# Constants, modulation head, norm, features and the q, k, v projection in one stage

## The reference

```python
cs = jax.nn.silu(c)
mod = cs @ ada_w[l] + ada_b[l]                       # 1024 -> 6 * 1024
sh1, sc1, gt1, sh2, sc2, gt2 = split(mod, 6)
h = rmsnorm(x, norm_g[l, 0]) * (1.0 + sc1) + sh1
z = h @ mix_in[e]                                    # 1024 -> 3584
qb, kb, vb = split(z[..., 2048:], 3, -1)             # 512 columns each
qb = rope(qb, pos); kb = rope(kb, pos)
```

## Time and profile before

| | |
|---|---|
| median of 3 runs | 2945.14 us (2944.81, 2945.14 and one of 3172.86) |
| profiled execution | 2942.27 us, its span 2940.4 us |
| mean granted TensorE clock | 0.951 |
| busy in the span | TensorE 2632.1, VectorE 1587.1, ScalarE 1127.0, GpSimd 943.1 us |
| first load of the columns, of the head, of x, of the q, k, v stage | 2.25, 12.03, 50.08, 91.68 us |
| first instruction of the stage behind | 275.83 us |

### The profile page before, as it was taken

How to read it: one execution, slowest core, us unless ns; L and a number is a source line. 1 busy time by engine, 2 the same in 40 slices (tenths; PEclk the granted TensorE clock), 3 DMA queues, 4 the chain that set the end, 5 groups by cost and what they waited for, 6 DMA issues and landing times. The chain is left out here.

```text
span 2940.4 us, 54937 instructions
## 1 busy us (share of the span) xinstructions
PE 2632.1 (90%) x23160; PEld 2148.2 (73%) x23160; DVE 1587.1 (54%) x2286; ACT 1127.0 (38%) x1791; POOL 943.1 (32%) x645
## 2 busy tenths in 40 slices
PE   2688999796899999996999999999797999999998
PEld 0466755464889888775888888877575888888887
DVE  4565642255565454564655556445745655556445
ACT  1311243353333333343444444445343444444434
POOL 0510212101112111212777772000232677774000
PEclk7899999898999999998999999999798999999999
DMA  5556634602311211322222226643132222225654
GB/s 174 183 198 221 209 129 179 215 21 62 89 46 53 83 46 68 109 73 72 74 85 79 86 86 220 193 157 126 67 108 86 65 86 86 76 82 186 204 186 148
DMA packets 299010, 346.50 MB, mean 118 GB/s; under 512 B 31485, under 2 KB 227290, under 8 KB 298766
## 3 DMA queue, kind: packets, MB, share of 16 engines
q1 hardware_dynamic: 289118, 336.65, 35.3%
q10 hardware_dynamic: 9648, 6.34, 0.7%
HBM read 271.59 MB, written 71.35 MB: 117 GB/s over the span
## 5 line engine op out<-in xcount | busy, mean ns | idle before, releaser
L2835 POOL TENSOR_TENSOR cg_u_lo<-cg_u_raw,cg_u_hi 128x512 fp32r<-128x512 f32 x216 | 328.0, 1526 | 139.2 <-ACT cg_u_hi L2721 139.2
L307 PE MATMUL cg_ps<-m_hi,cg_u_hi 128*128 128x512 f32 x844 | 331.7, 393 | 32.7 <-POOL cg_u_lo L2835 28.4
L309 PE MATMUL cg_ps<-m_hi,cg_u_lo 128*128 128x512 f32 x844 | 330.4, 392 | 0.0
L308 PE MATMUL cg_ps<-m_lo,cg_u_hi 128*128 128x512 f32 x808 | 316.1, 391 | 0.0
L2721 ACT ACTIVATE cg_u_hi<-cg_u_raw 128x512 fp32r<-128x512 f32 x216 | 132.2, 629 | 387.4 <-PE cg_ps L309 235.1
L307 PEld LDWEIGHTS cg_ps<-m_hi,cg_u_hi 128*128 128x128 f32 x844 | 159.9, 189 | 68.0 <-POOL cg_u_lo L2835 29.2
L2885 DVE SCALAR_TENSOR_TENSOR cg_z<-cg_ps,top_conv_f,cg_z 128x1023 f32<-128x1023 f32 x88 | 112.9, 1283 | 137.1 <-ACT cg_z L2745 137.1
L307 PE MATMUL cg_ps<-over_y_tx,cg_u_hi 128*128 128x512 f32 x480 | 186.8, 389 | 0.0
L308 PE MATMUL cg_ps<-over_y_tx,cg_u_hi 128*128 128x512 f32 x480 | 186.8, 389 | 0.0
L309 PE MATMUL cg_ps<-over_y_tx,cg_u_lo 128*128 128x512 f32 x480 | 186.8, 389 | 0.0
L309 PEld LDWEIGHTS cg_ps<-m_hi,cg_u_lo 128*128 128x128 f32 x844 | 159.8, 189 | 33.5
(11 more groups left out here) (468 smaller groups left out, 6492.2 us busy)
## 6 DMA issues: line engine op xcount, KB each, us to landing
cg_u_raw<-in_ffn_up SPq DMA_DIRECT2D x88, 512.0 KB, 5.4
cg_u_raw<-in_ffn_down SPq DMA_DIRECT2D x64, 512.0 KB
qkv_mw<-in_ada_w SPq DMA_DIRECT2D x12, 2048.0 KB
over_f_d_raw<-in_ffn_down SPq DMA_DIRECT2D x48, 512.0 KB
scr_act<-cg_z SPq DMA_DIRECT2D x44, 512.0 KB, 2.7
mod_w<-in_ada_w SPq DMA_DIRECT2D x8, 1024.0 KB
za_w_raw<-in_mix_in SPq DMA_DIRECT2D x16, 512.0 KB, 4.9
za_out<-in_ada_w SPq DMA_DIRECT2D x8, 1024.0 KB
```

What stands on the lines that cost most here:

```text
L307: nc.tensor.matmul(out, a_hi, b_hi, start=first, stop=False)
L308: nc.tensor.matmul(out, a_hi, b_lo, start=False, stop=False)
L309: return nc.tensor.matmul(out, a_lo, b_hi, start=False, stop=last)
L2835: G.tensor_tensor(u_lo[:, n % RING], source(g, i), u_hi[:, n % RING].bitcast(F32), ALU.subtract).then_inc(ulo_done, 1)
```

## The change

The five stages become one, `features_and_qkv`, without a barrier in between. `columns` has 19 groups: the biases of shift and scale and the norm's gain come as columns too. SP loads in the order of `HEAD_ORDER`: halves of head chunks and pairs of token tiles in turns, the 19 groups behind chunk 1. The head uses the stream's two weight slots. VectorE adds up one chunk at a time and scales a token tile when its turn comes. The sum over partitions takes the accumulator as weights, 128 columns at a time, against the column of ones, so shift and scale arrive as columns in PSUM and do not pass through HBM. Inverse roots come from a root on ScalarE and a reciprocal on VectorE. TensorE turns each token tile by itself, ScalarE evicts it to `xt`. Gain and shift are applied to whole rows of 1024 tokens, on ScalarE for h_hi and on VectorE for h32, and VectorE alone makes h_lo. h_hi lies over x, h_lo over xt. The rope tables are loaded behind w_raw 3. TensorE multiplies the first four tiles together, k by k as the low parts come.

```diff
-def modulation_head(nc, c, ada_w, ada_b, mod_d, consts):
...
-def norm_to_features(nc, name, x_src, norm_row, mod_row, at, consts, h_hi, h_lo):
...
-def project_qkv(nc, mix_in, h_hi, h_lo, consts, rope_cos, rope_sin, qk_d, v_d, ada_w, ada_b, mod_d):
+def features_and_qkv(nc, x_src, cond, mix_in, columns, x, xt, h_hi, h_lo, consts, rope_cos, rope_sin, qk_d, v_d, ada_w, ada_b, mod_d):
...
+            rows, sq = o.sb("rows", [max(sizes), 24, P]), o.sb("sq", [P, D])
+            h32 = Scope(nc, octx, "over_rope").sb("h32", [P, 4, D])
+        mps = s.ps("mps", [P, 2, CHUNK])
+        ms = ModulationStream(nc, s, 2, consts, modulation_room(s, 2) + (mps,))
-        ms = ModulationStream(nc, s, 2, consts, modulation_room(s, 2) + (s.ps("mps", [P, 2, CHUNK]),))
...
+        def x_bank(t):
+            return ps[:, 2 * (t % 2):2 * (t % 2) + 2, :].rearrange("p a (f c) -> p (a f) c", c=P)
+        HEAD_ORDER = [("w", 0, 0), ("w", 0, 1), ("x", 0), ("x", 1), ("w", 1, 0), ("w", 1, 1), ("x", 2), ("x", 3), ("w", 2, 0), ("w", 2, 1),
+                      ("x", 4), ("x", 5), ("w", 3, 0), ("x", 6), ("x", 7), ("w", 3, 1)]
...
             def load_chunk(c):
                 if c < 2:
                     sp.wait_ge(ms.pad_clear, 1)
+                    sp.wait_ge(row_done, HEAD * KT)
                 else:
                     sp.wait_ge(ms.acc_done, c - 1)
                 l, e = chunk_of(c)
                 ms.load(sp, ada_w[l].rearrange("(t p) (e n) -> e p t n", p=P, n=CHUNK)[e],
                         ada_b[l, e * CHUNK:(e + 1) * CHUNK].rearrange("(o n) -> o n", o=1), c % 2)
-            sp.dma_start(cos[:, :, :], rope_cos.rearrange("(t p) e -> p t e", p=P)).then_inc(tab_loaded, 16)
-            sp.dma_start(sin[:, :, :], rope_sin.rearrange("(t p) e -> p t e", p=P)).then_inc(tab_loaded, 16)
+            def head_chunk(j, half):
+                k = slice(half * KH, (half + 1) * KH)
+                if j >= 2:
+                    sp.wait_ge(row_done, (j - 2) * KT + (half + 1) * KH)
+                sp.dma_start(ms.w[:, j % 2, k], ada_w[0].rearrange("(t p) (e n) -> e p t n", p=P, n=CHUNK)[j][:, k]).then_inc(head_loaded[j][half], 16)
+            sp.dma_start(ccol[:, :], cond.rearrange("o (t p) -> p (o t)", p=P), allow_slow_non_contiguous=True).then_inc(c_loaded, 16)
+            for n, (kind, *at) in enumerate(HEAD_ORDER):
+                if kind == "w":
+                    head_chunk(*at)
+                else:
+                    sp.dma_start(x[:, at[0], :], x_src[at[0] * P:(at[0] + 1) * P, :]).then_inc(x_loaded[at[0]], 16)
+                if n == 5:
+                    for i, (src, _) in enumerate(columns):
+                        sp.dma_start(rows[0:sizes[i], i, :], src).then_inc(cols_loaded[i], 16)
             for n in range(NC * KT):
                 cb, k = divmod(n, KT)
...
                 if n >= R:
                     sp.wait_ge(lo_done, n - R + 1)
                 sp.dma_start(w_raw[:, n % R, :], w_v[k, :, 4 * WA + cb * WA:4 * WA + (cb + 1) * WA]).then_inc(raw_loaded[n % R], 16)
+                if n == R - 1:
+                    sp.dma_start(cos[:, :, :], rope_cos.rearrange("(t p) e -> p t e", p=P)).then_inc(tab_loaded, 16)
+                    sp.dma_start(sin[:, :, :], rope_sin.rearrange("(t p) e -> p t e", p=P)).then_inc(tab_loaded, 16)
                 if n == 2 * KT - 1:
                     for c in range(4):
                         load_chunk(c)
...
         def _(act):
+            A = nc.scalar.activation
+            def weight_high(cb, k):
+                n = cb * KT + k
+                act.wait_ge(raw_loaded[n % R], 16 * (n // R + 1))
+                A(w_hi[:, cb % 2, k, :], w_raw[:, n % R, :], ACT.Copy).then_inc(hi_done, 1)
-                    nc.scalar.activation(w_hi[:, cb % 2, k, :], w_raw[:, n % R, :], ACT.Copy).then_inc(hi_done, 1)
+                    weight_high(cb, k)
+            def square(t):
+                act.wait_ge(x_loaded[t], 16)
+                if t:
+                    act.wait_ge(ss_done, t)
+                A(sq[:, :], x[:, t, :], ACT.Square, accum_out=ss[:, t:t + 1]).then_inc(ss_done, 1)
+                act.wait_ge(ss_done, t + 1)
+                A(root[:, t:t + 1], ss[:, t:t + 1], ACT.Sqrt, scale=1.0 / D, bias=eps[:, :]).then_inc(root_done, 1)
+            def evict(t):
+                act.wait_ge(xs_turned, t + 1)
+                A(xt[:, :, t * P:(t + 1) * P], x_bank(t), ACT.Copy).then_inc(xt_done, 1)
+            def feature_high(f):
+                act.wait_ge(gain_done, 1)
+                act.wait_ge(shift_done, 1)
+                A(h_hi[:, f, :], xt[:, f, :], ACT.Identity, scale=gain[:, f:f + 1], bias=shift[:, f:f + 1]).then_inc(fhi_done, 1)
             def stage_out(cb, t):
                 n = cb * TT + t
...
+            act.wait_ge(eps_set, 1)
+            for t in range(TT):
+                square(t)
+                if t:
+                    evict(t - 1)
+            evict(TT - 1)
+            for k in range(R):
+                weight_high(0, k)
+            act.wait_ge(xt_done, TT)
+            for f in range(KT):
+                feature_high(f)
+                if f + R < KT:
+                    weight_high(0, f + R)
             split(1)
             for cb in range(NC):
                 for t in range(TT):
...
         @block.gpsimd
+            nc.gpsimd.memset(ident[:, :], 0.0).then_inc(zeroed, 1)
+            nc.gpsimd.memset(eps[:, :], RMS_EPS).then_inc(eps_set, 1)
+            pool.wait_ge(zeroed, 1)
+            nc.gpsimd.affine_select(out=ident[:, :], in_=ident[:, :], compare_op=ALU.not_equal, fill=1.0, base=0,
+                                    pattern=[[-1, P]], channel_multiplier=1).then_inc(ident_set, 1)
+            for n in range(NC * KT):
+                cb, k = divmod(n, KT)
+                pool.wait_ge(hi_done, n + 1)
+                nc.gpsimd.tensor_tensor(w_lo[:, cb % 2, k, :], w_raw[:, n % R, :], w_hi[:, cb % 2, k, :].bitcast(F32),
+                                        ALU.subtract).then_inc(lo_done, 1)
...
+            def head_rows(j, half):
+                dve.wait_ge(head_loaded[j][half], 16)
+                acc = ms.acc[:, j % 2, :]
+                for k in range(half * KH, (half + 1) * KH):
+                    w = ms.w[:, j % 2, k, :]
+                    if k:
+                        dve.wait_ge(row_done, j * KT + k)
+                        V.scalar_tensor_tensor(acc, w, silu[:, k:k + 1], acc, ALU.mult, ALU.add).then_inc(row_done, 1)
+                    else:
+                        if j >= 2:
+                            dve.wait_ge(chunk_summed, j - 1)
+                        V.tensor_scalar(acc, w, silu[:, 0:1], None, ALU.mult).then_inc(row_done, 1)
+            def scale_x(t):
+                dve.wait_ge(root_done, t + 1)
+                V.reciprocal(rstd[:, t:t + 1], root[:, t:t + 1]).then_inc(rstd_done, 1)
+                dve.wait_ge(rstd_done, t + 1)
+                V.tensor_scalar(x[:, t, :], x[:, t, :], rstd[:, t:t + 1], None, ALU.mult).then_inc(xs_done, 1)
+            def copy_columns():
+                dve.wait_ge(cols_turned, len(columns))
+                for i, (_, dst) in enumerate(columns):
+                    V.tensor_copy(dst, pt[:, 0, starts[i]:starts[i] + sizes[i]]).then_inc(cols_copied, 1)
+            def feature_low(f):
+                dve.wait_ge(h32_done, f + 1)
+                dve.wait_ge(fhi_done, f + 1)
+                V.tensor_tensor(h_lo[:, f, :], h32[:, f % 4, :], h_hi[:, f, :].bitcast(F32), ALU.subtract).then_inc(flo_done, 1)
             def chunk_rows(c):
                 dve.wait_ge(ms.loaded[c % 2], 32 * (c // 2 + 1))
                 if c >= 2:
                     dve.wait_ge(ms.sum_done, c - 1)
+                else:
+                    dve.wait_ge(chunk_summed, HEAD)
...
                 for k in range(KT):
                     ms.add_row(dve, c, c % 2, k)
+            V.memset(ones[:, :], 1.0).then_inc(ones_set, 1)
+            V.memset(heads[:, :], 0.0).then_inc(heads_zeroed, 1)
+            dve.wait_ge(heads_zeroed, 1)
+            V.memset(heads[0:HD, 0:HD], 1.0)
...
+            for n, (kind, *at) in enumerate(HEAD_ORDER):
+                if kind == "w":
+                    head_rows(*at)
+                else:
+                    scale_x(*at)
+                if n == 9:
+                    copy_columns()
+            dve.wait_ge(chunk_summed, HEAD)
+            dve.wait_ge(cols_copied, len(columns))
+            V.tensor_tensor(shift[:, :], mps[:, 0, 0:KT], shift_b[:, :], ALU.add).then_inc(shift_done, 1)
+            V.tensor_tensor(scale[:, :], mps[:, 0, KT:2 * KT], scale_b[:, :], ALU.add).then_inc(scale_done, 1)
+            dve.wait_ge(scale_done, 1)
+            V.scalar_tensor_tensor(gain[:, :], scale[:, :], 1.0, g[:, :], ALU.add, ALU.mult).then_inc(gain_done, 1)
+            dve.wait_ge(gain_done, 1)
+            dve.wait_ge(xt_done, TT)
+            for f in range(KT):
+                if f >= 4:
```

(59 more changed lines are left out.)

265 lines of the change are left out of this document (41 added, 224 removed).

## The result

The changed kernel takes 2911.26 us (median of four runs, 2908.25 to 2916.52) against 2945.14 of the kernel before (three runs, 2944.81 to 2948.07): 33.9 us less. The ratio is 0.9881, with a 95% interval of 0.9862 to 0.9900. That is 1.2% less, and by the 2% of the forecast no change. A fourth run of the kernel before, 3172.86 us in a slower state of the chip, is left out of all of this. The profiled execution took 2908.25 us with a span of 2906.5, against 2942.27 and 2940.4: 34 us less. The forecast was 2899, from a gain of 46.0 us at tile 4.

The account below looks back on a forecast made before the run. Serialization of five stages bounds until 108.5 us, then TensorE. First product gains 57.6 us, a new hole takes back nearly 12: 46.0 off 2942.27 gives 2896.3, plus 2.9 to the median, 2899; range 2886 to 2914.

Parts of the forecast that it names:

- the new hole: Before tile 4: TensorE idle some ten us, behind chunk 0's load and rows and rope 2; takes back nearly 12 us.
- low parts over 2.7 us apart: Sign of a wrong forecast, in the features: low parts coming slower than TensorE's 2.7 us for one k.
- Transfers and the head: Start to gain: transfers end at 37.1, VectorE and ScalarE bind, last half chunk ends at 45.6, gain at 47.5.
- rival (c): Head: late slot gates stall SP's stream, column sums cost 2.6 us more; gain 32 to 35, median 2910 to 2913; chance 0.11.
- Features: Behind the gain: low parts every 1.9 us, TensorE starts at 50.9, 57.6 us earlier, and is never held again.
- the lock: Features: VectorE operations wait for GpSimd's w_lo; one wait a pair makes the period 3.2, tile 4 1.8 us later.
- Four tiles: First four token tiles on TensorE: 4 x 5.45 us plus 1.7 lost at low clock, done at 74.4.
- Behind tile 4: Tile 4 to stage's end: same waits, 141 us; the chunk 4 hole moves along, could at most vanish (8.7 us).
- (d): TensorE stays at 1.2 GHz behind the hole before tile 4; for all 20 tiles 52 us slower, 2997; chance 0.03.
- rival (b): Features and head: VectorE waits for GpSimd, root and evictions later; 2 to 6 us lost, median 2901 to 2905; 0.70 with forecast.
- rival (a): VectorE follows transfers, chunk 0 in time, clock high at both starts: tile 4 at 79.0, gain 55.5, median 2890; chance 0.14.
- Rival (e): Head not on the path; gain given back at chunk 4 through waits tied to absolute time; 2945; chance 0.02.

Follow-up runs that it names:

- e11_columns: e6_both with VectorE's 19 column copies in the head moved from before the scaling of x4 to behind that of x5; 2895.21 us.
- e9_short_rows: Changed kernel with rows 1 to 7 of head chunks 1 and 3 multiplied on 32 of 512 columns only; 2917.05 us.
- e1_small_lo: Changed kernel with GpSimd's w_lo of column blocks 0 and 1 done on 32 of 512 columns; 2904.67 us.
- e0_same: The changed kernel run once more, unedited, beside the edited ones; 2910.08 us.
- e2_order: Changed kernel with the rows of streamed chunks summed one token tile later, so rope 2 precedes chunk 0's rows; 2900.37 us.
- e7_chunk4: Changed kernel with streamed chunk 4 asked for ahead of w_raw 20 instead of behind w_raw 23; 2907.12 us.
- e6_both: Changed kernel with streamed chunk rows one token tile later and block 0's w_lo moved from GpSimd to VectorE; 2894.58 us.
- e8_all: Changed kernel with the edits of e6_both and e7_chunk4 together; 2896.65 us.

## Why the prediction was right, and which step failed

The kernel became faster by less than 2%, as forecast, the new hole came for the reason given, and one price was wrong. Of the signs that the forecast gave for being wrong one came: low parts over 2.7 us apart.

**Transfers and the head: right in its times, not in what binds it.** Chunk 0's rows ended at 13.0 (forecast 12.5), the last rows at 45.5 (45.6); the column transposes took 2.35 us for 19, 0.12 each against 0.25. The four column sums, for which the forecast took the small end, were 1.84 us, in eight matmuls, at the low clock. The gain came 1.2 us late, 0.7 of it because its last operation already ran beside GpSimd (0.90 instead of 0.17). Up to chunk 1 the landings came as forecast; x2, behind the 19 column loads that were put at 1 us, was there at 21.6 and not at 19.7, and x4 at 29.6 and not at 27.8. So the claim that VectorE and ScalarE bind the head held in part: their chain through x4 does, as e11_columns shows, but it hangs on the transfer of x2 (e9_short_rows). The slot gates of rival (c) held nothing back: VectorE did not wait for the rows of chunks 2 and 3.

**Features: the step that failed.** "The rows of the low parts come every 1.9 us" and "it is never held again". They came every 3.9 us, and TensorE, once started, waited four times, 2.6 us in all. The forecast had the lock, from the earlier trace rows, and priced it at one w_lo a pair (a period of 3.2), beside the sum and not in it. It is one wait for each operation, two a pair. First product 54.4 instead of 50.9. GpSimd had eight w_lo of block 0 and eight of block 1 ready to do in just this stretch; its work "beside" was the term to look at. e1_small_lo prices the lock at 8.4 us at tile 4, of which 0.8 is the faster column sums.

**Four tiles: 82.9 instead of 74.4**, 3.5 from the start, the rest from the period of 3.9 (over TensorE's 2.7). The length of the low clock had no part in it that shows at tile 4. In the changed kernel's trace the products are 0.43 us apart, as at the low clock, until 60.5, 6 us where the earlier trace rows had shown 3.5 (its granted clock reads 1.00 there, and falls for the first time shortly before 88); in e0_same the granted clock is 0.50 only until 58.2, and tile 4 starts at 94.69 all the same.

**The new hole: right in kind, smaller.** Tile 4 was released by the rope of tile 2, behind chunk 0's rows, as forecast, and e2_order shows it. The wait of 2.4 us for chunk 0's load did not occur: VectorE came 8.5 us later than forecast and the load was there. In e1_small_lo, where VectorE came at 74.1, it did wait, 0.8 us. So of the 8.5 us late, tile 4 shows 6.2 (94.7 instead of 88.5).

**Behind tile 4: right.** From tile 4 to the stage's end 140.8 us; forecast 141. The hole at chunk 4 came again, 7.6 us on TensorE where it had been 8.7. That it could be had for nothing by SP's order (e7_chunk4) the forecast mentioned as a bound of 8.7; 6.1 came.

**The sum.** 46.0 - 6.2 (the lock, and some 0.5 of slower column sums) + 0.6 (shorter distance) = 40.4 at the stage's end. From there the forecast counted on 0, and 6.5 went in the profiled execution: 1.0 at the restart of the next stage, 3.9 in it by the clock, 1.6 further back, where two traces of one kernel differ as much. The forecast had this rival, (d), only as tiles of its own stage at the low clock. By the medians 33.9 us (2945.1 - 2911.3) of the 46.0 arrived. It was rival (b)'s mechanism, and more of it than (b) had been given (2901 to 2905); with what was lost up to the stage's end alone the median would have been 2904.7. That the measured 2911 lies in the forecast's range of 2886 to 2914 is luck in part: the range reaches beyond 2905 only for rival (c), whose mechanism did not occur, and the 6.5 us lost behind the stage, for which the forecast had no term, took its place. Of rival (a) one part came, chunk 0 in time, and only because VectorE was late. Rival (e) fell: nothing behind tile 4 was tied to absolute time.

## What to carry to other kernels

Before VectorE work is moved, list what GpSimd does at that time: with both queues full each VectorE operation had to wait for one of GpSimd's (0.81 to 1.77, 1.22 to 2.30 us), so moving GpSimd's part to VectorE had VectorE done 11.6 us sooner, though it got 5.2 us more work, and GpSimd 1.4 us later (77.2 instead of 75.8). The features were what TensorE waited for. Where tiles are finished together, look at what stands between them in the consumer's program order; here one number in the schedule of the streamed chunks was worth 9.7 us. e6_both, with both edits, is the fastest version found, beside e11_columns and e8_all, which cannot be told from it.

## What the runs showed of the hardware

- GpSimd's subtraction on 128x512, when it ran beside them, lengthened four kinds of VectorE operation: scaling on 128x1024 by 1.0 us, subtraction by 1.1, the rows of a chunk by 0.9, the 128x8 gain by 0.7.
- The granted clock in unchanged code differed with the code ahead of it, by some us of time: a stage of 264.0 and 264.8 us took 266.3 to 268.6. A gain measured at one stage's end need not reach the span: 40.4 us there, 33.9 at the end.
- Behind the same pause of 7.80 us TensorE stayed at the low clock for different times: its first tile took 5.96 us in the changed kernel, 6.44 in e0_same, which is the same program, and 6.93 in e9_short_rows.
- A kernel with less work (e9_short_rows) took 5.8 to 7.0 us longer. No run shows why.
